# A decoder step with dilated attention: the three branches of each KV head in reversed order

## The chip, the core and the metric

The kernel runs as one program on 1 core of a Trainium2 chip. The metric is the time of the program on the device in microseconds (us). Three runs of the kernel before the change took 2828.98, 2829.54 and 2831.64 us, so the median is 2829.54 us. The engines are named PE (TensorE, matmuls and transposes), DVE (VectorE), ACT (ScalarE), POOL (GpSimd, here it only issues DMAs) and SP (SyncE, issues DMAs).

## The reference, cut to what matters

One step of a two-layer decoder for a prompt of 1024 positions and 32 sample positions: a state-space layer and an MLP, then dilated sliding-window attention and an MLP. The attention has three branches (window, dilation), each with 4 KV heads of size 64 and 4 query heads per KV head.

```python
BRANCHES = ((128, 1), (512, 4), (2048, 16))
...
def dilated_mixer(h, pos, kv_branches, kv_past, w_q, w_o):
    q = rope((h @ w_q).reshape(n, t, N_BRANCH, HEADS_PER_BRANCH, HEAD_DIM), pos)
    for g, (win, dil) in enumerate(BRANCHES):
        ...                       # scores, mask, softmax, values of one branch
        outs.append(o)
        lses.append(l)
    wts = jax.nn.softmax(jnp.stack(lses, axis=0), axis=0)
    o = jnp.einsum('gnth,gnthe->nthe', wts, jnp.stack(outs, axis=0))
    return o.reshape(n, t, ATTN_OUT).astype(h.dtype) @ w_o
```

The three branches of a head are independent of each other until their outputs are mixed with weights that come from the three log-sum-exps. So the order in which they are computed is free.

## The kernel before, in words

The attention phase for the prompt (`attention_phase`) goes through 12 pairs of a KV head g and a branch b, n = 0 to 11. `head_branch(n)` says which pair has number n: before, it is head n // 3 and branch n % 3, so each head has branch 0 (local), 1 and 2 (widest) in turn. Each pair has two kinds of work.

First, 12 items (`KIND`): three chunks of the projection of K and V ("kv"), three of the first two query heads ("q0"), a transpose of V ("vt"), three chunks of the other queries ("q1"), a transpose of K for the output ("kt") and one for the sample rows ("st"). Each projection chunk is 24 matmuls (L2259 to L2261). DVE rotates the projected rows (`rotate`, L2139 to L2163), rescales and splits the weights (L1521, L1529); ACT copies PSUM to SBUF (L2043) and rounds the weights (L1525).

Second, 8 steps, one for each tile of 128 query positions (t = 0 to 7); step u is tile u % 8 of pair u // 8, and there are 96. A step is: `score` on PE (L2274, 4 matmuls), `maxima` on DVE (L2188 x4, then L2192, which writes ML), `exps` on ACT (L2056 x4), `turn_p` on PE (transposes of P, L2288), `keep_p` on ACT (L2066) and on DVE (L2200), `values` on PE (L2301), `keep_o` on ACT (L2073). A tile looks at one or at two blocks of 128 keys, and `keys(b, t)` says which: branch 0 has two blocks in 7 of its 8 tiles, branch 1 in 4 of 8, branch 2 in none. A step with two blocks is called wide below, the other narrow.

The order of the work is written out by hand, the same for each engine: in iteration u PE does `score(u + 1)`, the items of u, `turn_p(u)`, `values(u - 1)`. The items run 18 ahead: pair n's steps hide the items of pair n + 1 and the first half of those of n + 2. The last item stands in iteration 83, so iterations 84 to 95 (the second half of pair 10, and pair 11) have steps alone. From iteration 90 each also has one group of transposes for the sample part (L1859), and DVE spreads the sample queries (L1888).

The branches are mixed while later steps run (`Mixing`). When a head's 24 steps are over, POOL stores the maxima and sums (L1594) and loads them back in another order in 16 small DMAs (L1605, L1607); positions x = 0 to 30 after that are tied to the step number (`mixing(u)`): POOL loads outputs and weights (L1625, L1628), DVE computes weights (L1644 to L1667), multiplies (L1683) and adds (L1690). Position x = 28 of one head falls in iteration 52 or 76, the fifth step of pair 6 or 9. For the last head SP issues the 16 loads instead, after the last step, and the sample phase waits for them (L1644) before PE goes on (L2591).

POOL also stores K and V of the outputs (`kv_out`, L1970, L1975): 1 DMA each for branch 0, 8 for branch 1 and 8 for branch 2 (`kept_tiles`, `N_PARTS`). SP loads the sample cache (KVR, L2360, L2363) as soon as the last item is over.

Of the kernel before, what the change touches and what calls it, by code (L numbers as in the profile page):

```python
# [1439 lines left out]
def by_tile(ap, b, n):  # L1440

    if b == 2:
        return ap
    if b == 1:
        return ap.rearrange("p (s e i) -> p e s i", e=2, i=64) if n else ap.rearrange("p (e s i) -> p e s i", e=2, i=64)
    return ap.rearrange("p (t r i) -> p r t i", t=8, r=8) if n else ap.rearrange("p (r t i) -> p r t i", t=8, r=8)
# [29 lines left out]
N_PARTS = (1, 2, 1)  # L1476


def head_branch(n):

    return n // 3, n % 3


def kept_tiles(b):

    return [t for t in range(NTT) if b == 2 or (b == 1 and t % 2 == 1) or (b == 0 and t == 7)]
# [8 lines left out]
class ColTiles:  # L1495
# [8 lines left out]
    def load(self, sp, c):  # L1504
        (g, b), kind = head_branch(c // 3), c % 3
        dst = self.s.raw[:, c % 2]
        if kind == 0:
            for x in range(2):
                lo = 512 * b + 256 * x + 64 * g
                sp.dma_start(dst[:, :, 64 * x:64 * x + 64], self.wkv[:, :, lo:lo + 64]).then_inc(self.w_in[c % 2], 16)  # L1510
        else:
            lo = 1024 * b + 256 * g + 128 * (kind - 1)
            sp.dma_start(dst, self.wq[:, :, lo:lo + 128]).then_inc(self.w_in[c % 2], 16)
# [379 lines left out]
def attention_phase(nc, m, block, s, a, outs, w, norm, mlp, mix, keys_s):  # L1893
# [7 lines left out]

    def k_stores(n):

        return sum(N_PARTS[i % 3] * len(kept_tiles(i % 3)) for i in range(n))

    def group(u):
        return (*head_branch(u // 8), u % 8)
# [48 lines left out]
    def swaps(c):  # L1956
        return 16 * sum(2 if i % 3 == 0 else 4 for i in range(c % 2, c + 1, 2))

    @block.gpsimd
    def _(pool):  # L1960
        def kv_out(n, kind):
            g, b = head_branch(n)
            e = slice(64 * g, 64 * g + 64)
            ov = outs[5 + b].rearrange("n t x h e -> (n t) x (h e)")
            first = SEQ - min(BR[b][0], SEQ)
            if kind == "vt":
                pool.wait_ge(kept, N_IT * n + 7)
                for t in kept_tiles(b):
                    for dst, part in tile_rows(outs[2 + b][0][:, 1].rearrange("t h e -> t (h e)")[:, e], b, t, first):
                        pool.dma_start(dst, s.v[part, n % 3, t, :]).then_inc(v_st, 16)  # L1970
            elif kind == "kt":
                pool.wait_ge(kept, N_IT * n + 11)
                for i, t in enumerate(kept_tiles(b)):
                    for dst, part in tile_rows(outs[2 + b][0][:, 0].rearrange("t h e -> t (h e)")[:, e], b, t, first):
                        pool.dma_start(dst, s.kout[part, i, :]).then_inc(k_st, 16)  # L1975
            else:
                pool.wait_ge(kept, N_IT * n + 12)
                pool.dma_start(ov[:, 1, e], s.vn[32 * b:32 * b + 32, e]).then_inc(new_st, 16)
                pool.dma_start(ov[:, 0, e], s.sout[:]).then_inc(new_st, 16)
# [7 lines left out]
        for u in range(N_STEPS + 1):  # L1987
            if u == N_STEPS:
                mix.pool_maxima(pool, 3)
            if 0 < u:  # L1990
                g, b, t = group(u - 1)
                pool.wait_ge(o_kept, u)
                pool.dma_start(s.od[g, b][:, :, t], s.ot[:, (u - 1) % RO]).then_inc(o_st[(u - 1) % RO], 16)
            if u < N_STEPS:
                items(items_of(u))
            if u == 84:
                pool.wait_ge(prj, N_GR * N_IT)
                keys_s.zero_queries(pool, 0, a["c_zero"])
            if u == 87:
                pool.wait_ge(roped, 3 * N_GR)  # L2000
                for part in range(1, 3):
                    keys_s.zero_queries(pool, part, a["c_zero"])
            for x, g in mixing(u):
                if x == 12:
                    for i in range(RO):
                        pool.wait_ge(o_st[i], 16 * o_stores(24 * g + 24, i))
                mix.pool_part(pool, x, g)
            if u == 90:
                pool.wait_ge(k_st, 16 * k_stores(N_GR))
                pool.wait_ge(v_st, 16 * k_stores(N_GR))  # L2010
                pool.wait_ge(new_st, 32 * N_GR)
                mix.pool_rows(pool, 2, mix.made, 3)

    @block.scalar
    def _(act):
        def keep(i):
# [3 lines left out]
            if kind == "vt":  # L2020
                if n >= 3:
                    act.wait_ge(v_st, 16 * k_stores(n))
                    act.wait_ge(pv, 8 * (n - 2))
                nc.scalar.activation(s.v[:, n % 3].rearrange("p t e -> p (t e)"), ps[:, i % 3, :], ACT.Copy).then_inc(kept, 1)
            elif kind == "kt":
                if n:
                    act.wait_ge(k_st, 16 * k_stores(n))
                w_ = 64 * len(kept_tiles(b))
                nc.scalar.activation(s.kout[:].rearrange("p t e -> p (t e)")[:, 0:w_], ps[:, i % 3, 0:w_], ACT.Copy).then_inc(kept, 1)
            elif kind == "st":  # L2030
                if n:
                    act.wait_ge(new_st, 32 * n)
                if n % 3 == 2 and n > 2:
                    mix.act_keep(act, n // 3 - 1, ps[0:96, i % 3, 128:256])
                nc.scalar.activation(s.vn[32 * b:32 * b + 32, 64 * g:64 * g + 64], ps[0:32, i % 3, 64:128], ACT.Copy)
                nc.scalar.activation(s.sout[:], ps[0:32, i % 3, 0:64], ACT.Copy).then_inc(kept, 1)
            else:
                c = 3 * n + ("kv", "q0", "q1").index(kind)
                x = (j - (0, 3, 7)[c % 3])
                if x == 0 and c >= 2:  # L2040
                    act.wait_ge(roped, c - 1)
                lo, k = CHUNKS[x]
                nc.scalar.activation(s.qa[:, c % 2, lo:lo + k], ps[:, i % 3, 0:k], ACT.Copy).then_inc(kept, 1)  # L2043
# [58 lines left out]
    def _(dve):  # L2102
# [12 lines left out]
        def turn_by(c, part):  # L2115

            qa, qb = s.qa[:, c % 2], s.qb(c)
            if part == 0:
                dve.wait_ge(swapped[c % 2], swaps(c))
                nc.vector.tensor_tensor(qa[:], qa[:], s.rope[:, 0], ALU.mult).then_inc(turned_by, 1)  # L2120
            elif part == 1:
                nc.vector.tensor_tensor(qb[:], qb[:], s.rope[:, 1], ALU.mult).then_inc(rotated, 1)
            else:
                dve.wait_ge(turned_by, 1)
                dve.wait_ge(rotated, c + 1)
                b = c // 3 % 3
                nc.vector.tensor_tensor(by_tile(s.qt[:, 1, 1], b, 1), by_tile(qa[:, 0:SEQ], b, 0), by_tile(qb[:, 0:SEQ], b, 0), ALU.add)
                nc.vector.tensor_tensor(s.qs[:, b, 7], qa[:, SEQ:NT], qb[:, SEQ:NT], ALU.add).then_inc(roped, 1)

# [81 lines left out]
        for u in range(N_STEPS):  # L2211
            if u + 1 < N_STEPS:
                maxima(u + 1)
            for i in items_of(u):
                item(i)
            keep_p(u)
            for x, g in mixing(u):
                mix.dve_part(dve, x, g)
            if 84 <= u < 87:
                turn_by(3 * N_GR - 1, u - 84)  # L2220
            if 92 <= u:
                for r in range(2):
                    keys_s.put_queries(dve, (u - 92) // 2, u % 2, r)
            if u >= 90 and keys_s.by_dve(u - 90):
                keys_s.keep_dve(dve, u - 90)
# [603 lines left out]
```

## Time and profile before

| | us |
|---|---|
| median of 3 runs | 2829.54 |
| the profiled execution | 2831.03 |
| its span | 2829.2 |
| PE busy in the span | 2676.9 (95%) |
| DVE busy | 1366.5 (48%) |
| ACT busy | 838.4 (30%) |
| first `score` of the attention phase | 1232.8 |
| end of the last `values` | about 1862.7 |

A row of the timeline gives the start, the duration, the engine, the line and the operation, what is written and read, the count, and in brackets the idle time of the engine before it with what ended it. The matmuls are pipelined, so the distance between two starts is what one group costs PE, not the duration. PEclk is the granted clock of TensorE as a share of 2.4 GHz; 0.5 is 1.2 GHz.

### The profile page before, as it was taken

The page shows a single profiled execution, that of the slowest core. Times are in us where ns is not written, and L with a number is a line of the kernel's source. Part 1 is how long each engine was busy: PE and PEld are TensorE (multiplying, and loading weights), DVE is VectorE, ACT ScalarE, POOL GpSimd, SP SyncE. Part 2 cuts the span into 40 slices and gives each one's busy share as a digit, 9 for nine tenths or more (in the row PEclk, how much of TensorE's full clock was granted, in tenths as well). Part 3 has the DMA queues.
Part 4 walks back from the last instruction along what each step waited for, and adds up shares of the span by engine and source line. Part 5 has one row for each costly group of instructions (what it writes and reads, how often), then busy time and mean ns, then how long its engine had stood idle before and what let it go on. Part 6 is the DMA issues. An engine that isn't in the chain of part 4 may idle for free.

```text
span 2829.2 us, 44427 instructions
## 1 busy us (share of the span) xinstructions
PE 2676.9 (95%) x18634; PEld 2550.0 (90%) x18634; DVE 1366.5 (48%) x2264; ACT 838.4 (30%) x1690; POOL 266.7 (9%) x435
## 2 busy tenths in 40 slices
PE   5589999999999999999999999979999999999998
PEld 4479999999999999988888888747999999999998
DVE  7982235423332333766666767656354333233325
ACT  7241132111111112345555555543131111111212
POOL 2200000000000000012132424320000000000000
PEclk7789999999999999999999999999999999999999
DMA  3512111111111111323334545477111111111101
GB/s 97 80 37 60 45 45 45 38 46 51 44 44 44 44 44 38 108 69 78 81 77 123 135 115 131 154 262 268 45 45 45 45 44 44 44 44 44 44 30 62
DMA packets 174927, 208.43 MB, mean 74 GB/s; under 512 B 47382, under 2 KB 129734, under 8 KB 174136
## 3 DMA queue, kind: packets, MB, share of 16 engines
q1 hardware_dynamic: 149904, 158.10, 18.5%
q0 software_dynamic: 20272, 47.15, 6.0%
q10 hardware_dynamic: 4608, 1.18, 0.4%
q8 instruction: 100, 1.64, 0.2%
q14 instruction: 43, 0.35, 0.0%
HBM read 159.88 MB, written 27.82 MB: 66 GB/s over the span
## 4 chain that ended last, share of the span: by engine, by line
PE 76%; DVE 7%; ACT 3%; issue 2%; DMA 2%; POOL 1%; SPq 0%; DVEq 0%; ACTq 0%
PE PS L221 12%; PE PS L218 12%; PE PS L217 11%; PE PS L396 8%; PE PS L400 8%; PE PS L397 8%; PE PS L2259 4%; PE PS L2260 4%; PE PS L2261 4%; PE PS L2274 2%; PE PS L2301 1%; PE PS L2288 1%; DVE SSB L2188 1%; DVE SQ L191 1%; DVE TMP L328 1%
## 5 line engine op out<-in xcount | busy, mean ns | idle before, releaser
L217 PE MATMUL PS<-XH,WH 128*128 128x352 f32 x1920 | 617.4, 322 | 3.8 <-PEq L103 3.8
L218 PE MATMUL PS<-XL,WH 128*128 128x352 f32 x1920 | 618.8, 323 | 0.0
L396 PE MATMUL PS<-HIDH,WH 128*128 128x352 f32 x1536 | 494.7, 323 | 8.1 <-DVE HIDL L331 8.1
L397 PE MATMUL PS<-HIDL,WH 128*128 128x352 f32 x1536 | 494.6, 323 | 0.0
L221 PE MATMUL PS<-XH,WL 128*128 128x352 f32 x1920 | 414.9, 324 | 0.0
L217 PEld LDWEIGHTS PS<-XH,WH 128*128 128x128 f32 x1920 | 362.2, 189 | 4.1 <-issue 4.0
L218 PEld LDWEIGHTS PS<-XL,WH 128*128 128x128 f32 x1920 | 361.0, 188 | 0.1
L347 DVE TENSOR_TENSOR H<-PS,H 128x1056 f32<-128x1056 f32 x128 | 160.9, 1257 | 390.8 <-PE PS L400 390.5
L400 PE MATMUL PS<-HIDH,WL 128*128 128x352 f32 x1536 | 331.5, 324 | 0.0
L221 PEld LDWEIGHTS PS<-XH,WL 128*128 128x128 f32 x1920 | 329.4, 188 | 0.0
L396 PEld LDWEIGHTS PS<-HIDH,WH 128*128 128x128 f32 x1536 | 289.2, 188 | 12.7 <-DVE HIDL L331 12.7
L2259 PE MATMUL PS<-XH,AWH 128*128 128x384 f32 (+1 forms) x864 | 287.9, 333 | 2.1 <-DVE XL L171 2.0
L397 PEld LDWEIGHTS PS<-HIDL,WH 128*128 128x128 f32 x1536 | 288.3, 188 | 0.0
L328 DVE TENSOR_TENSOR TMP<-TMP 128x1056 f32<-128x1056 f32 x64 | 80.6, 1259 | 421.0 <-ACT TMP L291 420.8
L282 ACT ACTIVATE WH<-RAW 128x2048 fp32r<-128x2048 f32 x60 | 114.5, 1908 | 559.7 <-PE PS L400 559.7
L2260 PE MATMUL PS<-XL,AWH 128*128 128x384 f32 (+1 forms) x864 | 279.8, 324 | 0.0
L2261 PE MATMUL PS<-XH,AWL 128*128 128x384 f32 (+1 forms) x864 | 279.4, 323 | 0.0
L400 PEld LDWEIGHTS PS<-HIDH,WL 128*128 128x128 f32 x1536 | 263.2, 188 | 0.0
L2056 ACT ACTIVATE SSB<-SSB,ML 128x128 f32<-128x128 f32 (+1 forms) x384 | 168.4, 440 | 175.9 <-DVE ML L2192 175.8
L291 ACT ACTIVATE TMP<-PS 128x1056 f32<-128x1056 f32 x64 | 67.4, 1053 | 478.6 <-PE PS L221 478.6
L2259 PEld LDWEIGHTS PS<-XH,AWH 128*128 128x128 f32 x864 | 162.8, 188 | 16.7 <-issue 10.2
L2260 PEld LDWEIGHTS PS<-XL,AWH 128*128 128x128 f32 x864 | 163.0, 189 | 0.0
(387 smaller groups left out, 3393.2 us busy)
## 6 DMA issues: line engine op xcount, KB each, us to landing
RAW<-w_up SPq DMA_DIRECT2D x32, 1024.0 KB, 5.3
RAW<-w_down SPq DMA_DIRECT2D x32, 1024.0 KB, 4.8
KVR<-cache_kv_w SPq DMA_DIRECT2D x18, 1024.0 KB, 13.0
QB<-QA SPq DMA_DIRECT2D x120, 132.0 KB, 2.5
ARAW<-w_q SPq DMA_DIRECT2D x24, 512.0 KB, 4.7
O_SCRATCH<-OT POOLq DMA_DIRECT2D x96, 128.0 KB, 3.0
OB<-O_SCRATCH POOLq DMA_DIRECT2D x24, 512.0 KB, 7.0
RAW<-w_glu SPq DMA_DIRECT2D x16, 512.0 KB, 4.9
```

The lines of the kernel that those rows point to most:

```text
L217: nc.tensor.matmul(out, wh(k), xh[:, k, c], start=(k == 0), stop=False)
L218: nc.tensor.matmul(out, wh(k), xl[:, k, c], start=False, stop=False)
L221: mm = nc.tensor.matmul(m.ps[:, bank + t, 0:TW], wl(k), xh[:, k, c], start=False, stop=(k == kn - 1))
L282: nc.scalar.activation(m.wh[:, j % 2, :], m.raw[:, j % 2, :], ACT.Copy).then_inc(w_hi, 1)
L347: nc.vector.tensor_tensor(hv, banks(m, f % 2), hv, ALU.add).then_inc(added, 1)
L396: nc.tensor.matmul(out, w, m.hidh[:, k, q], start=(k == 0), stop=False)
L397: nc.tensor.matmul(out, w, m.hidl[:, k, q], start=False, stop=False)
L400: mm = nc.tensor.matmul(m.ps[:, 3 * (f % 2) + t, 0:TW], wl[:, 512 * k + o:512 * k + o + 128], m.hidh[:, k, q], start=False, stop=(k == 3))
L2056: ins = nc.scalar.activation(p, p, ACT.Exp, scale=0.125, bias=s.ml[:, g, b, t, 0, r:r + 1], accum_out=s.ml[:, g, b, t, 1, r:r + 1])
L2259: nc.tensor.matmul(out[:, 0:z], wh, m.xh[:, k, lo:lo + z], start=(k == 0), stop=False)
L2260: nc.tensor.matmul(out[:, 0:z], wh, m.xl[:, k, lo:lo + z], start=False, stop=False)
L2261: mm = nc.tensor.matmul(out[:, 0:z], wl, m.xh[:, k, lo:lo + z], start=False, stop=(k == KT - 1))
```

## The change

`head_branch(n)` now gives branch 2 - n % 3, so each head has branch 2, 1 and 0 in turn. Two places that spelled the order out are brought in line.

```diff
 def head_branch(n):
-    return n // 3, n % 3
+    return n // 3, 2 - n % 3
...
     def k_stores(n):
-        return sum(N_PARTS[i % 3] * len(kept_tiles(i % 3)) for i in range(n))
+        return sum(N_PARTS[b] * len(kept_tiles(b)) for b in (head_branch(i)[1] for i in range(n)))
...
-                b = c // 3 % 3
+                b = head_branch(c // 3)[1]
```

Pairs 0, 3, 6 and 9 turn from branch 0 to branch 2 (from 7 wide steps to none), pairs 2, 5, 8 and 11 from branch 2 to branch 0; pairs 1, 4, 7 and 10 stay. The positions of the mixing are tied to the step number and stay too.

The instructions of DVE around position x = 28 (iterations 76 and 77, pair 9), before: PTS is P transposed, SSB the masked scores, CB and OB the accumulator and the output that the mixing multiplies, QA, QB, QT the rotated queries.

```order
L2200 COPY PTS<-PS 128x512
L1683 TENSOR_TENSOR CB<-OB,CB 128x1024
L2188 ISA SSB,MX<-PS,MASK 128x256
...
L2192 TENSOR_SCALAR ML<-MX 128x4
L2146 TENSOR_TENSOR QA<-QA,ROPE 128x1056
L2147 TENSOR_TENSOR QB_130<-QB_130,ROPE 128x1056
L2156 TENSOR_TENSOR QT<-QA,QB_130 128x2x8x64
L2157 TENSOR_TENSOR QS<-QA,QB_130 128x32
```

The same place now:

```order
L2200 COPY PTS<-PS 128x2x128
L1683 TENSOR_TENSOR CB<-OB,CB 128x1024
L2188 ISA SSB,MX<-PS,MASK 128x128
...
L2192 TENSOR_SCALAR ML<-MX 128x4
L2146 TENSOR_TENSOR QA<-QA,ROPE 128x1056
L2147 TENSOR_TENSOR QB_130<-QB_130,ROPE 128x1056
L2156 TENSOR_TENSOR QT<-QA,QB_130 128x2x8x64
L2157 TENSOR_TENSOR QS<-QA,QB_130 128x32
```

The multiplication of the mixing stands where it stood, between the same neighbours; only the steps around it are narrow now.

PE in iterations 88 and 89 (transposes and values of steps 87 to 89, scores of 89 and 90), as a difference:

```order
-L2274 MATMUL PS<-KTD,QT 128x128 x4
+L2274 MATMUL PS<-KTD,QT 128x256 x4
 L2288 MATMUL PS<-IDENT,SSB 128x128 x4
 L2301 MATMUL PS<-PTS,V 64x256 x4
-L2274 MATMUL PS<-KTD,QT 128x128 x4
-L2288 MATMUL PS<-IDENT,SSB 128x128 x4
+L2274 MATMUL PS<-KTD,QT 128x256 x4
+L2288 MATMUL PS<-IDENT,SSB 128x128 x8
 L2301 MATMUL PS<-PTS,V 64x256 x2
```

Steps 89 to 95, which have no items beside them, are wide now: 256 columns in each score, 8 transposes and 4 value matmuls where there were 4 and 2.

## Rows read from the trace of the kernel before

**Rows 1.** The page, its first line: the span of the profiled execution.
```profile
span 2829.2 us, 44427 instructions
```
**Rows 2.** Waits of PE, from 1225 to 1822 us: us, times, longest.
```profile
PE PS L2274 <- DVE ML L2192: 6.7, 7, 2.4
```
**Rows 3.** Windows, PE alone: pair 3 (branch 0), then pair 5 (branch 2).
```profile
1408.23:1467.68 59.45, 59.45 (x417) 1.00 0.37 77
...
1523.77:1575.86 52.09, 51.24 (x356) 1.00 0.58 150
```
**Rows 4.** Timeline of PE, a wide step of pair 3.
```profile
1424.42 1.04 PE L2288 MATMUL PS<-IDENT,SSB 128*128 128x128 f32 x8
1425.39 1.08 PE L2301 MATMUL PS<-PTS,V 128*64 128x256 f32 x8
1426.40 1.13 PE L2274 MATMUL PS<-KTD,QT 64*128 64x256 f32 x8
1427.47 0.44 PE L2259 MATMUL PS<-XH,AWH 128*128 128x384 f32 x1
```
**Rows 5.** Timeline of PE, a narrow step of pair 2.
```profile
1376.86 0.60 PE L2288 MATMUL PS<-IDENT,SSB 128*128 128x128 f32 x4
1377.39 0.65 PE L2301 MATMUL PS<-PTS,V 128*64 128x256 f32 x4
1377.97 0.71 PE L2274 MATMUL PS<-KTD,QT 64*128 64x128 f32 x8
1378.62 0.44 PE L2259 MATMUL PS<-XH,AWH 128*128 128x384 f32 x1
```
**Rows 6.** Lines by form, 1150 to 1900 us: busy us, mean ns, idle before.
```profile
L2056 ACT ACTIVATE SSB<-SSB,ML 128x256 f32<-128x256 f32 x176 | 87.3, 497 | 96.2 <-DVE ML L2192 96.2
...
L2056 ACT ACTIVATE SSB<-SSB,ML 128x128 f32<-128x128 f32 x208 | 81.0, 392 | 79.7 <-DVE ML L2192 79.6
...
L2188 DVE CUSTOM_DVE_ANT_0 SSB<-PS,MASK 128x256 f32<-128x256 f32 x176 | 64.0, 419 | 25.1 <-PE PS L2274 25.0
...
L2188 DVE CUSTOM_DVE_ANT_0 SSB<-PS,MASK 128x128 f32<-128x128 f32 x208 | 47.8, 286 | 21.6 <-PE PS L2274 21.6
...
L2200 DVE COPY PTS<-PS 128x512 f32<-128x512 f32 x44 | 30.3, 688 | 29.0 <-PE PS L2288 28.9
...
L2200 DVE COPY PTS<-PS 128x256 f32<-128x256 f32 x52 | 22.0, 423 | 18.7 <-PE PS L2288 18.6
```
**Rows 7.** Waits of DVE, 1500 to 1822 us.
```profile
DVE CB L1683 <- DMA CB<-C_SCRATCH: 8.4, 4, 3.3
```
**Rows 8.** Timeline of POOL, pair 9: first load of maxima, weights for x = 28.
```profile
1752.73 0.65 POOL L1605 DMA_DIRECT2D ML<-ML_SCRATCH  x1 [1.64 <-DMA ML_SCRATCH<-ML]
...
1765.38 1.57 POOL L1628 DMA_DIRECT2D CB<-C_SCRATCH  x2
```
**Rows 9.** Timeline of DVE, pair 9, from the multiplication of x = 28 on.
```profile
1774.50 1.23 DVE L1683 TENSOR_TENSOR CB<-OB,CB 128x1024 f32<-128x1024 f32 x1 [2.32 <-DMA CB<-C_SCRATCH]
...
1788.78 1.23 DVE L1529 TENSOR_TENSOR AWL<-ARAW,AWH 128x1024 fp32r<-128x1024 f32 x1 [2.58 <-ACT AWH L1525]
...
1798.37 0.69 DVE L2200 COPY PTS<-PS 128x512 f32<-128x512 f32 x1
...
1800.55 0.41 DVE L2188 CUSTOM_DVE_ANT_0 SSB<-PS,MASK 128x256 f32<-128x256 f32 x1
...
1802.04 0.17 DVE L2192 TENSOR_SCALAR ML<-MX 128x4 f32<-128x4 f32 x1
```
**Rows 10.** Timeline of PE, the score that follows on it.
```profile
1802.26 0.49 PE L2274 MATMUL PS<-KTD,QT 64*128 64x128 f32 x4 [0.38 <-DVE ML L2192]
```
**Rows 11.** Windows: the clock's fall; steps 88 to 95 (busy PE, PEld, DVE, ACT, POOL).
```profile
1834.50:1838.00 3.50, 3.50 (x20) 2.19 (x18) 1.49 (x8) 2.40 (x10) 0.69 (x1) 0.51 1.04 425
1833.34:1862.64 29.30, 22.74 (x172) 14.11 (x172) 17.88 (x129) 21.86 (x91) 11.69 (x20) 0.94 1.04 405
```
**Rows 12.** Chain that ended last, after the last steps: start, us.
```profile
1862.85 4.81 DMA ML_SCRATCH<-ML
1867.71 0.69 SPq L1605
```

## The prediction

> **What bounds the kernel now.** I read the first line of the page [rows 1], then the waits of PE in the attention phase, then windows by pair, then the timelines of PE, DVE and POOL where PE waits, and last the chain of waits through the end of the phase. From the first score to iteration 83 PE hardly ever stops: it waits for the maxima (ML) 7 times, 6.7 us together, and the longest, 2.4 us, is at the start of the phase [rows 2]. So up to iteration 83 a pair costs what its PE work costs: 59.45 us for a pair with branch 0 and 52.09 us for one with branch 2, 51.24 of it busy [rows 3]. After that the steps have no items beside them and PE waits in between: of the 29.30 us of steps 88 to 95 it is busy 22.74 [rows 11]. Behind the last step the path leaves PE: the store of the last head's maxima takes 4.81 us, then 16 loads follow [rows 12].
>
> **What the change moves.** A wide step costs PE 3.05 us (1424.42 to 1427.47) and a narrow one 1.76 us (1376.86 to 1378.62) [rows 4, 5]. A pair that turns from branch 0 to branch 2 loses 7 x 1.29 = 9.0 us of PE work, one that turns the other way gains 9.0. The windows of rows 3 agree: 59.45 - 51.24 = 8.2 us, and the second window holds one wide score of the pair behind it. On DVE a wide step costs 4 x (419 - 286) ns = 0.53 us more in the maxima and 0.27 us more in the copy of P, on ACT 4 x (497 - 392) = 0.42 us more in the exponentials [rows 6].
>
> *PE work up to iteration 83.* Pairs 0, 3, 6 and 9 lose 36.0 us, pairs 2, 5 and 8 gain 27.0. That is -9.0 us, if PE stays the bound. The missing 9.0 is pair 11, which stands in the part without items.
>
> *The cover that pairs 3, 6 and 9 lose.* These three pairs are those in which DVE also makes the mixing weights, and 6 and 9 also hold position x = 28. While they had branch 0, PE was slow enough for DVE. Take pair 9. POOL spends its time from the end of pair 8 on stores and 16 loads of maxima, and issues the weights for x = 28 at 1765.38 only, behind the loads that begin at 1752.73 [rows 8]. They land at 1774.50, and DVE waits 2.32 us there already; the longest of the four such waits is 3.3 [rows 7, 9]. From there DVE is almost never idle until ML at 1802.04, and PE's score waits for that at 1802.26, with 0.38 us of idle time [rows 9, 10]. So landing to score is 27.8 us of DVE, with 2.58 us for ACT's rounding of weights in it. After the change that stretch loses two wide maxima, three wide copies of P and one wide group of exponentials: 2 x 0.53 + 3 x 0.27 + 0.42 = 2.3 us. PE loses 9.0. POOL's burst is tied to the output copy of the last step of the pair before, which comes 1.3 us sooner behind PE's position (0.53 in the maxima and 0.42 in the exponentials of a step that turns narrow, and some of PE's own wait there). So PE gains 2.3 + 1.3 = 3.6 us of its 9.0, and the other 5.4 us are a new wait for ML and for P on DVE's side, in pair 9 and, by the same pattern, in pair 6: +10.8 us. The bounds: 0 if the weights land much sooner, 2 x 7 = 14 if nothing of the 1.3 is had. I take 10.8, because the stretch is one continuous row of DVE work.
> Pair 3 has no position 28, but it has the weights: between the copy of P at 1798.37 and the next maxima at 1800.55 there are 2.18 us, of which the copy is 0.69 at most, so 1.5 or more are the weights [rows 9]. A branch 2 pair without mixing has almost no slack at its end (PE is busy 51.24 of 52.09 even in pair 5), so they show: +1.7, between 0 and 2.2.
> Pairs 5 and 8, now branch 0, lose their small waits at the end, about 0.85 [rows 3] and as much again by the sum in rows 2: -1.9. Pairs 1, 4 and 7 keep their steps; a wide score follows where a narrow one did: +0.2, between 0 and 1.
> The stores of K and V for the outputs move on POOL with their branch: the 8 and 8 of branch 2 go from the pair before 2, 5, 8 and 11 to the pair before 3, 6 and 9 and to the start. I cost that at nothing: in front of the burst of rows 8 stand the 8 of branch 1, as before. Behind branch 2's now stand the weights of position 17, which DVE takes two steps later; were they late, DVE would wait there as at x = 28, in a pair that is wide now and has room for it.
> Sum up to iteration 83: -9.0 + 10.8 + 1.7 - 1.9 + 0.2 = +1.8 us.
>
> *Steps 88 to 95.* They get the 9.0 us of PE work that came off the first part. In the 29.30 us of before PE idles 6.56 us [rows 11]. If the wide steps filled all of that, the part would grow by 2.4 us; if none, by 9.0. A wide step still leaves PE to wait: after the maxima come 2.0 us of exponentials (4 x 497 ns) before the transposes, and only the score of the next step, 1.07 us, stands before them on PE [rows 4, 6]. That leaves about 1 us of idle time in every second step, and the spreading of the queries on DVE stays. So I let PE idle 4.9 us instead of 6.56: +7.3, between +2.4 and +9.0.
>
> *Behind the last step.* The loads of the sample cache start with the last item and the DMA engines are full through steps 88 to 95 (share 1.04, 405 GB/s) [rows 11]. With 7 us more in these steps that backlog is gone before the store of the last maxima. The same store for head 2 left POOL waiting 1.64 us and no more [rows 8]; with its issue of about 0.6 us it takes some 2.2 us instead of 4.81: -2.6, and 0.1 more because the store hangs on the second to last output copy. -2.7, between 0 and -4.
> The Trainium skill ("DMA: Bandwidth & Descriptors", Anatomy of one DMA) has a DMA from POOL take about 2.0 us plus its bytes at 436 GB/s, which is 2.2 us for this store of 96 KB; that is an estimate from the page. By it the 4.81 us are queueing, and the term would be -2.6; a reading by which the store always costs 4.8 at this place would give 0 and a total of +10.1.
>
> *TensorE's clock.* It fell to 0.51 (1.2 GHz) at 1834.5 to 1838.0 [rows 11], after PE had idled in the steps without items, and 3.5 us of work took twice their time there, at most 1.7 us lost. The new waits of 2 us each in pairs 6 and 9 stand beside PE-bound work. I add one half-felt fall: +1.0, between 0 (none) and 3.4 (two in full).
>
> Total: +1.8 + 7.3 - 2.7 + 1.0 = +7.4 us on the profiled execution's 2831.03, whose span of 2829.2 makes up all but 1.8 of it; that run stands 1.5 above the median. On the median: 2829.54 + 7.4 = 2836.9, say 2837.
>
> **The rivals.** What a measurement of this kernel can tell from no change is 0.2%, or 5.7 us.
> *A, an exchange.* The waits in pairs 6 and 9 are small because the weights for x = 28 land sooner, since fewer or smaller transfers stand beside them. For it: those transfers are tied to POOL's burst and not to the branch, but each shares the DMA engines. Against it: POOL issues them at 1765.38 whatever the step's width. With 1.9 us of wait each instead of 5.4: 2837 - 7.0 = 2830.
> *B, the other side.* The wide steps at the end fill PE's idle time: the part grows by 2.4 instead of 7.3, and with A's small waits the total is 7.4 - 4.9 - 7.0 = -4.5, with no fall of the clock -5.5, so 2824; the kernel is no slower from the point at which pairs 6 and 9 wait less than 2 us each and the tail fills half of its idle time. For it: DVE is busy 17.88 of 29.30 there and ACT 21.86, so neither is full. Against it: the chain score, maxima, exponentials, transposes is a latency that no free engine shortens.
> *C, worse.* The tail keeps all its idle time (+9.0), the store behind it is as slow as before (0 for -2.7), and the clock falls twice in full (+3.4): 1.8 + 9.0 + 3.4 = +14.2, so 2844.
> *D, no change of order.* The rows of the order show other widths at the same places, so the change does what it says. No chance is kept for it.
>
> **How the numbers follow.** My forecast has 0.50, A 0.27, B 0.11, C 0.12. Slower by over 0.2% is nearly all of C, and of my forecast the part above 2835.2, which I put at 0.46: 0.58. Faster by over 0.2%, below 2823.9, is a good half of B: 0.07. The rest is 0.35. The range goes from between A and B to just short of C: 2827 to 2843.
>
> **What would show it.** In the profile of the changed kernel: waits of PE for ML and P (L2274 and L2288 for L2192 and L2200) that rise from 6.7 to about 17 us before iteration 84, at 2 us each, in pairs 6 and 9; DVE's wait for the weights at L1683 of 5 us or more at two places; the last item's end 1 to 3 us later than before, not 9 earlier; steps 88 to 95 in 36 to 37 us with PE busy near 32; the store of the last maxima in 2 to 3 us. If PE passes iteration 83 more than 5 us sooner than before, the step on pairs 6 and 9 is wrong, and so is the sign. If steps 88 to 95 take under 33 us, the step on their idle time is wrong.

## The result: 8.8 us slower, and the profile after

The changed kernel takes 2839.87 us (median of 6 runs, 2837.67 to 2845.24); the kernel before took 2832.07 in the runs beside it (6 runs, 2828.98 to 2832.82). The medians differ by 7.8 us. The ratio of the two sets of runs is 1.0031, with a 95% interval of 1.002 to 1.0043, which is +8.8 us (+5.7 to +12.2); this ratio is used below. The profiled execution took 2841.74 us, 10.7 more than the one of before.

The starts of chosen instructions in both traces, from the start of the span, say where it comes in (the output copy is `keep_o` on ACT, L2073, once a step):

| | before | after | after - before | added in this part |
|---|---|---|---|---|
| first score of the attention phase | 1232.79 | 1233.56 | +0.8 | +0.8 |
| output copy of step 83 | 1826.97 | 1833.67 | +6.7 | +5.9 |
| output copy of step 95 | 1862.66 | 1875.34 | +12.7 | +6.0 |
| first matmul of the w_o product | 1957.01 | 1967.51 | +10.5 | -2.2 |
| end of the span | 2829.2 | 2839.9 | +10.7 | +0.2 |

The +0.8 of the first row says nothing of the change: over the fourteen traces of this document the first score starts between 1231.4 and 1237.8 us, in either order of the branches.

The page's first line, against [rows 1]:

```profile
span 2839.9 us, 44427 instructions
```

The waits of PE between 1225 and 1825 us, against [rows 2] (us in total, times, longest):

```profile
PE PS L2274 <- DVE ML L2192: 12.6, 9, 2.4
PE PS L2288 <- DVE PTS L2200: 4.2, 3, 2.1
PE PS L2288 <- ACT SSB L2056: 0.5, 1, 0.5
```

They add up to 17.3 us. Before there were 7.7: the 6.7 for ML of [rows 2], and 1.0 for P, which [rows 2] leaves out. This is the row of before for P:

```profile
PE PS L2288 <- DVE PTS L2200: 1.0, 2, 0.6
```

The waits of DVE for the late weights, 1400 to 1822 us, against [rows 7], are fewer and longer:

```profile
DVE CB L1683 <- DMA CB<-C_SCRATCH: 11.8, 2, 6.8
```

The timeline of DVE has these two, the first in pair 6 and the second in pair 9 [rows 9]. The timeline of POOL has the first load of maxima of pair 9 and the weights for x = 28 [rows 8]:

```profile
1608.64 1.23 DVE L1683 TENSOR_TENSOR CB<-OB,CB 128x1024 f32<-128x1024 f32 x1 [6.83 <-DMA CB<-C_SCRATCH]
...
1782.39 1.23 DVE L1683 TENSOR_TENSOR CB<-OB,CB 128x1024 f32<-128x1024 f32 x1 [4.94 <-DMA CB<-C_SCRATCH]
```

```profile
1760.92 0.64 POOL L1605 DMA_DIRECT2D ML<-ML_SCRATCH  x1 [1.64 <-DMA ML_SCRATCH<-ML]
...
1773.56 1.55 POOL L1628 DMA_DIRECT2D CB<-C_SCRATCH  x2
```

From POOL's first load to the multiplication there are 21.5 us after and 21.8 before. This run of DMAs did not change; the steps that pass meanwhile became shorter, so DVE stands at the multiplication sooner. PE waits at the end of that row of work, as its timeline shows: the first two rows are pair 6, the last pair 9.

```profile
1630.92 0.63 PE L2288 MATMUL PS<-IDENT,SSB 128*128 128x128 f32 x4 [1.91 <-DVE PTS L2200]
1633.98 1.23 PE L2274 MATMUL PS<-KTD,QT 64*128 64x128 f32 x8 [1.85 <-DVE ML L2192]
...
1804.81 1.08 PE L2288 MATMUL PS<-IDENT,SSB 128*128 128x128 f32 x4 [2.12 <-DVE PTS L2200]
```

The rows behind such waits carry a second cost. 1804.81 took 1.08 us where the same transposes took 0.63 at 1630.92, and the score at 1633.98 took 1.23. The granted clock (third value from the right in the windows) says why:

```profile
1633.90:1637.20 3.30, 3.22 (x14) 3.00 (x15) 2.27 (x12) 3.24 (x12) 0.00 (x0) 0.50 0.00 0
1804.50:1811.30 6.80, 5.57 (x23) 4.21 (x24) 5.60 (x30) 3.45 (x14) 0.05 (x1) 0.50 0.00 1
```

At 0.50, or 1.2 GHz, PE does half its work in that time. Over wider windows of PE (PE, PEld, DVE, ACT and POOL busy, the clock, DMA share, GB/s), first before, then after:

```profile
1600.00:1640.00 40.00, 38.90 (x272) 34.10 (x271) 28.80 (x82) 18.84 (x62) 11.03 (x21) 1.00 0.42 110
1790.00:1820.00 30.00, 29.62 (x217) 26.12 (x215) 20.02 (x66) 13.16 (x46) 7.52 (x14) 1.00 0.23 67
```

```profile
1600.00:1640.00 40.00, 33.27 (x222) 30.00 (x219) 26.75 (x82) 15.08 (x59) 11.59 (x20) 0.96 0.47 120
1790.00:1820.00 30.00, 26.04 (x163) 22.68 (x161) 20.65 (x67) 12.85 (x47) 3.24 (x5) 0.89 0.18 52
```

40 x 0.04 + 30 x 0.11 = 4.9 us of full clock are missing after and none before. That is the most that these falls can cost, since PE idled in part of them.

Steps 88 to 95 against [rows 11], then the chain behind the last step against [rows 12]:

```profile
1839.86:1875.28 35.42, 30.14 (x228) 19.48 (x228) 24.23 (x132) 26.54 (x93) 11.26 (x19) 1.00 0.98 378
```

```profile
1874.94 2.11 DMA ML_SCRATCH<-ML
1877.11 0.69 SPq L1605
```

35.42 us instead of 29.30, PE busy 30.14 instead of 22.74, idle 5.3 instead of 6.6. The store takes 2.11 us instead of 4.81.

### The profile page after: what moved, and what is told of

Read it like the earlier page. It is cut to its first block, busy times and chain, and to the rows that moved or that the text cites. A ratio compares the mean times of both kernels' runs of the same rounds, so it can differ in the third digit from the quotient of the medians.

```text
span 2839.9 us, 44427 instructions
## 1 busy us (share of the span) xinstructions
PE 2680.2 (94%) x18634; PEld 2554.0 (90%) x18634; DVE 1367.0 (48%) x2264; ACT 838.4 (30%) x1690; POOL 266.6 (9%) x435
## 4 chain that ended last, share of the span: by engine, by line
PE 76%; DVE 7%; ACT 3%; issue 2%; DMA 1%; POOL 1%; SPq 0%; DVEq 0%; ACTq 0%
PE PS L221 12%; PE PS L218 11%; PE PS L217 11%; PE PS L396 8%; PE PS L400 8%; PE PS L397 8%; PE PS L2259 4%; PE PS L2260 4%; PE PS L2261 4%; PE PS L2274 2%; PE PS L2301 2%; PE PS L2288 2%; DVE SSB L2188 1%; DVE SQ L191 1%; DVE TMP L328 1%
## 5 line engine op out<-in xcount | busy, mean ns | idle before, releaser
L396 PEld LDWEIGHTS PS<-HIDH,WH 128*128 128x128 f32 x1536 | 289.2, 188 | 12.7 <-DVE HIDL L331 12.7
```

What stands on the lines that cost most here:

```text
L396: nc.tensor.matmul(out, w, m.hidh[:, k, q], start=(k == 0), stop=False)
```

## The experiments

The base of each is named in its text on record. Times are medians in us, ratios are to the kernel before in runs on the same chip (its medians there were 2832.98, 2833.84 and 2833.15), with the 95% interval. "Us against before" is the ratio's distance from 1 times 2833. An interval of 0.001 is 2.8 us.

### Which part of the order costs it

The last head alone reversed, and the other three alone:

```
-    return n // 3, 2 - n % 3
+    return n // 3, (2 - n % 3 if n >= 9 else n % 3)     # last head alone
+    return n // 3, (2 - n % 3 if n < 9 else n % 3)      # heads 0 to 2 alone
```

> Only the last head is reversed (pairs 9 to 11), heads 0 to 2 stand as before. Theory 1: pair 9 gives 9.0 us of PE work less and takes 3.6 to 5.4 back as waits, pair 11 costs 6 to 7 us more without items beside it, and the store behind it gives back 2 to 2.7: in all -2 to +2 us against the kernel before. Rival (all of the loss is in the last pair, whose steps nothing hides): +5 us or more.

Measured: 2833.09, ratio 1.0 (0.9991 to 1.0009), in the middle of the range expected.

> Heads 0 to 2 reversed, the last head as before, so the steps without items are the same as before and PE's work up to iteration 83 is the same too. Theory 1: pair 3 waits 1.5 us, pair 6 waits 5.5 us more, pairs 5 and 8 lose 1.9 us of waits: +4 to +7 us against the kernel before. Rival (all of the loss is in the last pair): within 1 us of the kernel before.

Measured: 2840.49, ratio 1.0026 (1.0015 to 1.0037), +7.4 us. The two parts, 0 and +7.4, make up the whole change's +8.8 within their intervals. +7.4 is just above the 4 to 7 expected. So the loss is in heads 0 to 2, where no PE work leaves the dense part and the stalls, with the falls of the clock behind them (3.4 us missing in the trace of this run from pair 1 on), are all that is left. In the last head several terms cancel. In the trace of the first of these two runs, PE's waits in pair 9 grow from 0.38 to 5.49 us and the clock stands at half for 6.8 us behind them, so the output copy of step 83 comes 594.2 us behind the first score before and 593.5 after, for all the 9.0 us of PE work that left; steps 84 to 95 take 6.0 us more, and the store behind them 2.7 less. A reading by which all of it is the slower tail falls.

### The late weights (position 28)

The multiplication and addition two positions later, the store one:

```
-        elif x in (23, 24, 28):
+        elif x in (23, 24, 30):
...
-        elif x in (25, 29):
+        elif x in (25, 31):
```

> The reversed order, with the multiplication of position x = 28 moved to x = 30, its addition from 29 to 31 and POOL's store from 30 to 31. Theory 1 (the weights that land late stall DVE in pairs 6 and 9, and PE behind it): DVE's waits at L1683 (6.8 and 4.9 us) go or fall under 2 us together, PE's waits in pairs 6 and 9 fall from about 10.6 to 3 us, and the kernel is 6 to 9 us faster than the reversed one: +1 to +3 us against the kernel before. Theory 2 (it is the narrow steps alone that leave DVE behind, whatever the weights do): DVE's waits go, but PE's waits fall by under 3 us and the kernel stays at +6 to +9 us.

Measured: 2836.99, ratio 1.0018 (1.0008 to 1.0028), so 3.7 us less than the reversed order by the ratios. The waits at L1683 are all gone, and still PE waits 11.9 us for ML. In pairs 6 and 9 its waits fell from 6.73 and 3.96 us to 3.5 and 3.7, and the longest is now 2.99. Neither theory has the size: at +5.1 us against before it lies between their ranges. The timelines of DVE and PE show why:

```profile
1623.79 0.41 DVE L2200 COPY PTS<-PS 128x256 f32<-128x256 f32 x1
1624.12 1.21 DVE L1690 TENSOR_TENSOR CB<-CB 128x1024 f32<-128x1024 f32 x1
1625.25 0.38 DVE L1659 TENSOR_TENSOR CC<-CC,ML 128x32 f32<-128x32 f32 x3
...
1626.51 0.42 DVE L1667 TENSOR_TENSOR COUT<-CC 128x32 f32<-128x32 f32 x3
1626.82 0.42 DVE L2188 CUSTOM_DVE_ANT_0 SSB<-PS,MASK 128x256 f32<-128x256 f32 x1
```

```profile
1628.54 1.22 PE L2274 MATMUL PS<-KTD,QT 64*128 64x128 f32 x8 [2.99 <-DVE ML L2192]
```

Position 31 is position 7 of the next head, where DVE also makes the weights (L1659 to L1667), in a pair's last step. The addition went into that block: one wait was exchanged for another.

> The same three positions moved in the order of before. Theory 1: only the two short waits of PE behind DVE in pairs 6 and 9 (1.1 and 0.4 us) can go: 0 to -1.5 us. Theory 2: the same, within 1.5 us of the kernel before.

Measured: 2833.22, ratio 1.0005 (0.9994 to 1.0015). In before's order the move gains nothing: the wide steps had covered most of the wait for the late weights. The two short waits did not go, as both theories had it; at the ends of pairs 6 and 9 PE now waits 1.93 and 2.15 us instead of 1.10 and 0.38.

### The block at a pair's end (position 7), and both

```
-        elif x == 7:
+        elif x == 8:
             self.dve_weights(dve, g)
```

> The reversed order, with DVE's weights of a head (seven small operations, L1658 to L1669) at position 8 instead of 7 of the mixing, so out of the step that ends a pair and into the first step of the next one. Theory (PE's wait for ML at the end of pairs 3, 6 and 9 is DVE's block of the pair's last step, of which the weights are a part): the wait of 1.5 us at the end of pair 3 goes, the last waits of pairs 6 and 9 (1.9 and 0.9 us) shrink, and the kernel is 2 to 4 us faster than the reversed one. Rival (the block is bound by the rope and the turned products, the weights only move to the next step where the wait shows again): the same within 1 us.

Measured: 2836.68, ratio 1.0009 (1.0 to 1.0018), 6.2 us under the reversed order by the ratios (3.2 by the medians of separate runs). The wait of 1.5 us at the end of pair 3 went, as expected; those for the late weights (12.8 us at L1683) stayed. The gain is above the 2 to 4 expected, by the ratios; the interval of a difference of two ratios is some 4 us to either side.

The multiplication and addition of the odd half one position later each, the store and the range with them, weights at 7:

```
-        elif x in (23, 24, 28):
+        elif x in (23, 24, 29):
...
-        elif x in (25, 29):
+        elif x in (25, 30):
```

> The reversed order with the multiply and the add of the odd half at positions 29 and 30 (store behind them), DVE's weights left at position 7. It parts the gain of 13 us that both moves together gave over the reversed order; the weights' move alone gave 3.2. Theory (the wait of DVE for the late weights and the block at a pair's end are two terms, and the two moves add up): 10 us under the reversed order, 2829 to 2832 against 2833 of before, with DVE's waits at L1683 near nothing and the waits of PE at the ends of pairs 3, 6 and 9 still there (1.5, and 1 to 2 us). Rival (the two moves only work together, since weights and multiply share the step at the pair's end): 4 to 6 us under it, 2834 to 2836.

Measured: 2834.21, ratio 1.0005 (0.9996 to 1.0014), 7.4 us under it by the ratios. The mirror of the run above: nothing is left at L1683, and the waits at the ends of pairs 3, 6 and 9 stay (1.5, 1.85 and 1.85 us). By the time alone this run decides nothing: 7.4 lies between the 10 of its theory and the 4 to 6 of its rival, and 2834.21 stands in the rival's range.

Both edits together:

> The reversed order, with the last multiply and add of an odd half of the mixing at positions 29 and 30 instead of 28 and 29 (one step later each, the store behind them too) and the weights at position 8 instead of 7. Theory (the stalls of pairs 6 and 9 are the late mixing weights, 6.8 and 4.9 us of DVE's wait at L1683, and moving them by two steps to 30 and 31 gained only 3.7 us because they then stood in the block at the pair's end beside DVE's weights): DVE's waits at L1683 fall to under 4 us in all, PE's waits for ML and P before iteration 84 fall from 16.8 to 5 to 9 us, and the kernel is 5 to 8 us faster than the reversed one, 2832 to 2835. Rival (what DVE must do in the four steps of the wide pair's end fits nowhere, the waits move along): PE's waits stay above 12 us and the gain is 3 to 4 us as it was with positions 30 and 31.

Measured: 2826.78, ratio 0.9974 (0.9965 to 0.9984), 7.4 us faster than before and 16.2 faster than the reversed order. The gain is twice what was expected. 6.2 + 7.4 = 13.6 is as near to 16.2 as the intervals tell. The traces are sharper: from the first score to the output copy of step 83 it takes 600.11 us in the reversed order, 593.36 with the weights moved, 593.15 with multiply and add moved, and 585.85 with both. That is 6.8 and 7.0 against 14.3 us less, on one execution each, so the two terms add up, and the rivals of a wait that moves along and of moves that only work together fall. Waits of PE, 1225 to 1822 us, of this kernel:

```profile
PE PS L2274 <- DVE ML L2192: 4.9, 5, 2.4
PE PS L2288 <- DVE PTS L2200: 1.4, 3, 0.7
PE PS L2288 <- ACT SSB L2056: 1.4, 2, 0.9
PE PS L2288 <- issue: 1.2, 2, 1.0
```

They fell from 17.3 to 8.9 us, by 8.4, and the output copy of step 83 comes 14.4 us sooner than in the reversed order. The rest is the clock, within 1.1 us. The same windows of this kernel, then the later one of the two kernels with one move each (positions 29 and 30, then weights at 8):

```profile
1600.00:1640.00 40.00, 39.20 (x268) 35.30 (x267) 32.19 (x95) 17.89 (x61) 10.07 (x18) 1.00 0.44 114
1790.00:1820.00 30.00, 27.07 (x202) 21.89 (x201) 20.03 (x79) 16.34 (x62) 6.29 (x11) 1.00 0.44 121
```

```profile
1790.00:1820.00 30.00, 27.40 (x187) 23.97 (x186) 18.48 (x60) 12.83 (x46) 3.24 (x5) 0.94 0.19 53
```

```profile
1790.00:1820.00 30.00, 27.79 (x184) 24.65 (x185) 20.27 (x63) 13.99 (x49) 3.93 (x6) 0.94 0.19 55
```

Clock missing in both windows together: 4.9 us reversed, 3.4 with either move (0.96 and 0.94), none with both. 8.4 + 4.9 = 13.3 of the 14.4 us.

### Both moves under each order

> The order of branches of the kernel before, with both moves (multiply and add at 29 and 30, weights at 8). It is the control: what the moves are worth where the wide branch comes first. Theory (the late weights wait only 3.3 and 2.3 us there, under wide steps that leave PE work to do; PE's waits for DVE before iteration 84 are 6.7 us in all, of which the pair ends 3, 6 and 9 hold little): 0 to 2 us faster than before, 2831 to 2833. Rival (the moves are worth as much in either order, and the reversed order gains nothing by itself): 7 to 13 us faster, 2820 to 2826.

> Both moves (multiply and add at 29 and 30, weights at 8) with the reversed order for the last head alone. Without the moves this order took 2833.1, the same as before, with 13.7 us of DVE's waits at L1683 in four places. Theory (within heads 0 to 2 the order gives nothing once the stalls are gone; in the last head eight wide steps leave the dense stretch ahead of iteration 84, where they cost their PE work, for the tail, where they cost 6 us): the stalls of pair 9 go and 2826 to 2830 is left, near the 2826.8 of all heads reversed with both moves. Rival (the gain of all heads reversed came from heads 0 to 2): 2830 to 2833.

> Both moves with heads 0 to 2 reversed and the last head in the order of the kernel before. Without the moves this order took 2840.5. Theory (the moves take back what the narrow pair 6 lost to waits, 6.7 us, and pair 3's 1.5; the last head stands as before): 2831 to 2834. Rival (the reversal pays in heads 0 to 2): 2824 to 2828.

With the run above these are four orders under both moves:

| heads 0 to 2 | last head | median | ratio (95%) | us against before | without the moves |
|---|---|---|---|---|---|
| as before | as before | 2830.76 | 0.9986 (0.9977 to 0.9995) | -4.0 | 0 |
| reversed | as before | 2829.79 | 0.9984 (0.9974 to 0.9995) | -4.5 | +7.4 |
| as before | reversed | 2826.60 | 0.9971 (0.9961 to 0.9982) | -8.2 | 0.0 |
| reversed | reversed | 2826.78 | 0.9974 (0.9965 to 0.9984) | -7.4 | +8.8 |

Heads 0 to 2 cost nothing once the moves are made (-0.5 and +0.8), and the last head brings 4.2 and 2.8 us, each about as large as the error of a difference of two such ratios (some 4 us). The first and the third row ran on the same chip and can be compared directly: their means differ by 3.5 us, give or take 2.4. Their traces say of what it is made. From the first score to the output copy of step 83 it takes 594.1 us with the last head as before and 586.2 with it reversed, 7.9 less; steps 84 to 95 take 35.6 and 41.7 us, 6.1 more; the store behind them takes 5.99 and 2.13. So the reversal pays little by itself, and only in the last head. The third run came in as its theory had it, the second row (2829.79) between the ranges of its theory and its rival. The moves are worth about 4 us in before's order, more than the 0 to 2 expected, with an interval of 1.4 to 6.5; the trace has 1.5 us of waits less (those of pairs 6 and 9), so part of the 4 may be chance. In the reversed order they are worth 16. Both versions with the last head reversed beat both kernels; they can't be told apart.

### The tail and the store behind it

Branch 0 of the last head takes one key block only; the keys of the second block are left out of its scores, softmax and values:

```
-        two = (b == 0 and t > 0) or (b == 1 and t % 2 == 1)
+        two = (b == 0 and t > 0 and g < 3) or (b == 1 and t % 2 == 1)
```

> The reversed order, with branch 0 of the last head alone taking one key block a step instead of two (the keys of the second block are left out of its scores, its softmax and its values; seven of its eight steps are meant). Nothing else is changed. Theory (the tail behind iteration 87 costs more because its eight steps are wide ones, 35.4 us where narrow ones took 29.3): steps 88 to 95 take 28 to 31 us, and the kernel is 5 to 8 us faster than the reversed one, near before's time. Rival (the eight last steps are slow for what stands beside them there, the sample's queries and keys on DVE, not for their width): they stay at 34 to 36 us and the kernel gains 1 to 2 us at most.

Measured: 2831.71, ratio 0.9998 (0.9988 to 1.0008), 9.3 us under the reversed order by the ratios, a bit more than expected. From the output copy of step 87 to that of step 95 it takes 20.4 us; the reversed order takes 27.6 and before 21.5. It is the width of the steps that costs, not what stands beside them. The store of the maxima, whose place in the queue is the same, became slow again:

```profile
1866.33 6.39 DMA ML_SCRATCH<-ML
```

In before's order, one load of the sample's keys behind the loads of the maxima on SP:

```
-        load(3, 4)
         sp.wait_ge(s.pv, N_STEPS)
         mix.load_maxima(sp, 3, mix.ml_late)
+        load(3, 4)
```

> The kernel before, in its own order of branches, with one transfer on SP's queue moved: the load (3, 4) of the sample's keys is issued behind the 16 loads of the last head's maxima instead of ahead of them. Theory (the 4.8 us store of the last maxima in the kernel before is the DMA engines being full of the sample's loads, since the same store took 2.11 us in the reversed order, 10 us later): if this one load is what fills them, the store takes about 2.2 us and the w_o product starts 1 to 2.6 us earlier, so 2830 to 2832 against 2833. Rival (the loads ahead of (3, 4), already under way, fill the engines, and the load that is moved was not in the way): the store stays at 4 to 5 us and the time stays within 1 us of before, or rises by up to 2 us since the moved load lands later.

Measured: 2835.99, ratio 1.0007 (0.9998 to 1.0016), no gain, and in its chain of waits the store is shorter, not short:

```profile
1869.22 3.78 DMA ML_SCRATCH<-ML
```

So my theory that this one load is all that is in the way falls; the rival is right on the time (+2.0), and the store is 1 us shorter than before, a bit less than it allowed. Over all fourteen traces the store took 2.1 us in the seven in which the last pair is wide and 3.8 to 6.4 us in the seven in which it is narrow. The DMA engines' share (last value but one) says what differs. The store starts at 1862.85 in the first window, of before, and at 1874.94 in the second, of the changed kernel:

```profile
1855.00:1865.00 10.00, 6.37 (x84) 4.09 (x84) 8.30 (x57) 7.00 (x26) 3.35 (x5) 1.00 1.05 405
1875.00:1885.00 10.00, 8.59 (x143) 7.19 (x140) 5.66 (x17) 3.25 (x7) 1.42 (x3) 1.00 0.20 43
```

In the 5 us ahead of the last output copy the share is 1.05 in each of the seven traces with the narrow pair and 0.50 to 0.64 in each of the seven with the wide one. So the slower tail lets the queued transfers finish before the store; which transfers they are was not shown.

## Why the prediction was right, step by step

2837 was forecast, 2839.87 was measured, slower by over 0.2%, and the stalls, the tail and the store came in where the steps put them. That the total is as near as this is partly luck: the clock cost 3 us more than was booked, and the tail 1.3 less, because a fall of the clock that before had there was gone. By its steps, on the profiled executions:

- *PE work up to iteration 83, -9.0.* It stands. Without stalls it shows as a gain: with both moves the output copy of step 83 comes at 1819.3, 7.7 us sooner than before. Against the kernel with the same two moves in before's order the stretch from the first score to there is 8.2 us shorter, with 0.7 us more of waits in it, so 8.9 us of PE work are gone.
- *Pairs 6 and 9, +10.8 as 5.4 each.* Right in mechanism. Idle time of PE in pair 6 went from 1.10 to 6.73 us (+5.6) and in pair 9 from 0.38 to 3.96 (+3.6), together +9.2. The stretch from the landing to the score is 25.3 and 25.5 us, 2.2 and 2.3 shorter, as the step had it. In pair 9 DVE waits 4.94 for the late weights, 1.9 less than in pair 6, and so less is left for PE. The experiments add what the step didn't see: DVE's block with the weights at the pair's end is as large a part of the loss as the late weights are (6.8 and 7.0 us, with the clock, when one of them is moved).
- *Pair 3, +1.7.* 1.5 (1458.56 to 1460.07), and it goes with the weights moved away.
- *Pairs 5 and 8, -1.9; pairs 1, 4 and 7, +0.2.* -1.9; and +0.1, since pairs 4 and 7 end with a wait of 0.98 us each now where they had 0.83 and 1.04, in two pieces each, for P and for ML.
- *Steps 88 to 95, +7.3.* The part of the change from step 83 to 95 is +6.0. It includes the fall of the clock at 1834.5 [rows 11], up to 1.7 us, that is gone after; without it the steps cost up to 7.7. Idle time of 5.3 us, forecast 4.9. PE is busy 30.14 us and not near 32, because the 22.74 of before held that half-clock stretch.
- *Behind the last step, -2.7.* -2.2; the store has its 2.7 in full (4.81 to 2.11). The Trainium skill ("DMA: Bandwidth & Descriptors", Anatomy of one DMA) makes this store 2.2 us, an estimate from its two figures; the trace agrees with the 2.11 where the last pair is wide, and no run with a narrow one reaches it.
- *TensorE's clock, +1.0.* Right in sign and mis-sized, the one term that was. From the first score to step 83 the kernel lost 5.9 us; the terms above are -9.0 + 9.2 + 1.5 - 1.9 + 0.1 = -0.1, so 6.0 us are left. The clock accounts for them: up to 4.9 us are missing in the two windows shown, and another half-clock stretch at the phase's start lasts 6.8 us instead of 3.4 (at most 1.7, with a new wait of 0.5 in it). This last part does not go with the order: the stretch lasts 6.8 us in twelve of the fourteen traces, in either order, and 3.4 only in that of before and in one other. The step said that the waits "stand beside PE-bound work" and booked half of a fall; each of pairs 6 and 9 had one, and that of pair 9 was twice as long. Less the 1.7 in the tail, the term is about +4.3, past the bounds of 0 to 3.4 that it named. It is also why the last item's end came 5.9 us later in this phase, where 1 to 3 had been forecast.

The sum by measured terms is 0.8 + 5.9 + 6.0 - 2.2 + 0.2 = 10.7 on the profiled executions and 8.8 by the ratio of the runs; forecast was 7.4. Rival A (small waits) and B (the tail absorbs the work) are both refuted by the windows above; C was right about the clock only.

## What to carry to other kernels

A long step that looks like pure cost can be the cover of a fixed run of work on another engine or of DMAs; before such steps are reordered, compare that run's length with the new length of the steps, and move the consumer along with them. When a stall is taken out, look at which block of the same engine comes next: here two terms of 6 to 7 us each had to go before the order, neutral or better by itself, showed its worth. Price a stall on TensorE at more than its length: here 10.7 us of new waits in pairs 3, 6 and 9 brought up to 4.9 us of missing clock with them.

## What the hardware showed that I had not expected

- Waits of about 2 us in a stretch in which PE was otherwise busy were followed by a fall of the clock, though not each time. After the waits of 1.91 and 1.85 us at 1629 to 1634 it stood at 0.50 for 3.4 us; around the wait of 2.12 us at 1802.7 for 6.8. The kernels whose waits there are at most 0.75 us have no such fall in pairs 6 and 9. With waits of 0.75 and then 1.85 there was one of 3.4 us each (1801.3, below). Before's order had waits up to 1.1 us in these pairs and no fall, and neither had the two runs with one of 1.4 in that order. But the reversed order's first wait of pair 6 (1.99 us, 1609.0 to 1611.0) had none, nor had one of 2.15 us in pair 9 of before's order with positions 30 and 31, while the 1.93 us of its pair 6 were followed by 3.4 us at half clock. With the weights at 8 alone the clock fell at 1610.8, behind a first wait of pair 6 of 1.74 us. What decides is open.

```profile
1797.98 0.63 PE L2288 MATMUL PS<-IDENT,SSB 128*128 128x128 f32 x4 [0.75 <-DVE PTS L2200]
1801.04 1.15 PE L2274 MATMUL PS<-KTD,QT 64*128 64x128 f32 x8 [1.85 <-DVE ML L2192]
```

```profile
1801.30:1804.70 3.40, 3.40 (x16) 3.18 (x15) 2.46 (x12) 3.40 (x15) 0.29 (x1) 0.52 0.00 0
```

- The same store of 96 KB took 2.1 us or 3.8 to 6.4 us at the same place in the program, by the width of the last eight steps ahead of it: 2.11 us became 6.39 when they alone were made narrow.
